# A one-core encoder layer with experts: order of evacuations, signals and idle products in the last attention steps and the last expert unit

## The chip, the core and the metric

The kernel runs on one core of one Trainium2 chip. The metric is the device time of the program in microseconds (us), lower is better. Five engines work beside each other, each through its own instructions in order: TensorE (PE, with its weight loads PEld), VectorE (DVE), ScalarE (ACT), GpSimd (POOL) and SyncE (SP), which here only issues transfers. They meet through semaphores: an instruction adds to one when it is done, another engine waits until the count is reached.

## What is computed

One layer on 1024 tokens of width 1024, in float32: a mixing part (four mLSTM heads, eight attention heads over a sliding window, one output projection), then a mixture of sixteen experts.

```python
x = x + jnp.concatenate([hm, ha], axis=-1) @ w_out[l]      # hm: mLSTM heads, ha: attention heads
x = x + hier_moe(rmsnorm(x, norm_ffn[l]), ...)             # top-1 group, top-2 experts in it
return rmsnorm(x, norm_final)
...
for e in range(N_EXPERTS):                                 # in hier_moe
    y = (jax.nn.silu(xt @ w_gate[e]) * (xt @ w_up[e])) @ w_down[e]
    out = out + combine[:, e:e + 1] * y
```

## The kernel before

**Products.** A float32 product is made of three rounded ones (`split3`, L1944 to L1946): both operands are split into a high part, which ScalarE writes as a rounded copy, and a low part, which VectorE writes as the difference. So every operand passes ScalarE, then VectorE, before TensorE may use it.

**Mixing part, steps.** After the input projection and the attention, a loop of steps s = 0 to 10 runs on all engines, with NT = 8 tiles of 128 tokens. In step s the mLSTM of tile s, the output projection of tiles s-2 (second 512 columns, `project(s-2, 1)`) and s-1 (first 512, `project(s-1, 0)`) and the router of tile s-3 go on. In `project(c, half)` the attention part comes first (`project_attention`: high rows AQH, made by `attention_hi(c)` on ScalarE at L1006, and low rows AQL, made by `attention_lo(c)` on VectorE at L1402), then from step 3 on the router's product `logits(c-2)` (L2152), then the mLSTM part (HTH from ScalarE at L1082, HTL from VectorE). In each step ScalarE first copies the two halves of the router's transposed rows (`router_evac`, L633; TensorE makes the second half only after `project(s-2, 1)`), then HTH, then AQH of tile s-1; further down it squares a tile for the norm (L1091) and the mLSTM's output (`sq`, L1096). VectorE waits in order for AQL, then adds a projection half to the residual (L1505), then makes HTL. Steps 7 and 8 have less TensorE work than those ahead: step 7 is the last with an mLSTM output and updates no state, step 8 does neither.

**From router to units.** After the last step VectorE makes tables of which token goes to which expert, in short steps that depend on each other (L1523 to L1564, L1659 to L1711); its last instruction, L1711, signals `s_tab`. TensorE fills waits with `keep_busy(n)`, n products of 128x128 that nobody reads (`ones` by the identity, L2231; each shows as two matmuls in the trace), reads two numbers of the table, transposes the first unit's rows (`x_half`, L2239) and begins the first unit's products.

**Expert units.** The sixteen units (at most 256 rows each, up to two halves of 128) each take six weight pieces of 1 MB: four for gate and up, j = 0 to 3, two for down, j = 4 and 5. SP loads a piece into RAW, ScalarE makes WH (L1069), VectorE makes WL (L1669, in the last unit L1733), TensorE multiplies. Three slots of WH and WL are used in turn, and `s_wused` counts the pieces that TensorE is through with. A unit's second half can be empty, full, or hold at most 64 rows ("few"): then both parts of these rows share one product (L2264, L2266). In this run the last unit has few rows in its second half.

**The last unit** is written apart. After piece j = 3 (up) come: ScalarE moves the lower half of the second half's up products (`low_rows(3)`, L1129 for SG); VectorE adds it (`both_rows`, L1766), multiplies by gate and silu (L1906 for the second half, `times_up(0, 1)`, L1772, for the first); TensorE transposes the hidden rows (L2308); ScalarE and VectorE split them into HH and HL (L1125, L1758); TensorE does piece j = 4 for both halves (12 matmuls each), adds the gathered rows of the tokens' sums by the identity (`add_rows`, L2396), and does piece j = 5. Beside this SP loads the eight tiles of 512 KB of the sum from device memory (`acc_dram`, L760), ScalarE squares them (L1235), VectorE scales them (L1919), SP stores them (L764), and at the very end POOL scatters the last unit's own rows over them (L931), in two halves, after all eight stores have landed.

Of the kernel before, what the change touches and what calls it, by code (L numbers as in the profile page):

```python
# [98 lines left out]
def build(nc, x, norm_mix, w_in, b_in, conv_qk, mlstm_norm, sinks, rel_bias, w_out, norm_ffn,  # L99
# [14 lines left out]
    with ctx:  # L114
# [822 lines left out]
        def _(act):  # L937
# [133 lines left out]
            for s in range(NT + 3):  # L1071
                if 3 <= s < NT + 2:
                    router_evac(act, s - 3, 0)
                    router_evac(act, s - 3, 1)
                if s == NT + 1:
                    router_evac(act, NT - 1, 0)
                    router_evac(act, NT - 1, 1)
                if 1 <= s <= NT:
                    act.wait_ge(s_ht, s)
                    if s >= 2:  # L1080
                        act.wait_ge(s_wo, 2 * s - 2)
                    A((hT0 if s == 1 else HTH)[:, :, :], PS[:, 3, :].rearrange("p (a b) -> p a b", a=4),  # L1082
                      ACT.Copy).then_inc(s_hte, 1)
                    if s >= 2:
                        attention_hi(s - 1)
                if 2 <= s < NT + 2:
                    c = s - 2
                    act.wait_ge(s_x2, 2 * c + 2)
                    if c >= 1:
                        act.wait_ge((s_xnst1, s_xnst0)[c % 2], 16 * ((c + 1) // 2))  # L1090
                    A(xnb[:, :], VM[:, c, 0:D], ACT.Square, accum_out=stat[:, c:c + 1]).then_inc(s_ss2, 1)  # L1091
                if s == NT + 1:
                    hi_piece(0, 0)
                if s < NT:
                    act.wait_ge(s_num, s + 1)
                    A(sq[:, 0:3, :], num3[:, :, 0:P], ACT.Square).then_inc(s_sq, 1)  # L1096
                if s + 1 < NT:
                    decays(s + 1)
                    scales(s + 1)
                if s == 1:  # L1100
                    act.wait_ge(s_wout, 32)
                    act.wait_ge(s_mog, 8)
                    for i in range(2):
                        A(WMH[i][:, :, :], wout[:, 2 * i:2 * i + 2, :], ACT.Copy).then_inc(s_wmh, 1)
# [117 lines left out]
            with act.If(second > 0):  # L1222
                with act.If(second < 2):
                    act.wait_ge(s_wused, 6 * u + 3 + SPLITS)
                    low_rows(2).then_inc(s_glo, 1)
                    gate_tanh(0).then_inc(s_th, 1)
                    act.wait_ge(s_gsum, 2 * u + GSUM + 1)
                    A(SG[0:FEW, 1, :], HB[0:FEW, 1, :], ACT.Tanh, scale=0.5).then_inc(s_th, 1)
                    act.wait_ge(s_wused, 6 * u + 4 + SPLITS)
                    low_rows(3).then_inc(s_glo, 1)  # L1230
# [5 lines left out]

            hi_piece(u, 5)
            for i in range(NT):
                if i == 2:
                    hi_piece(u, 6)  # L1240
                    hidden_hi(u, 0, 1)
                    hidden_hi(u, 1, 0)
                act.wait_ge(s_vm[i], 32)
                square(i, tile_of(i))
            act.wait_ge(s_dn1, u + 1)
            act.wait_ge(s_f2a, NT)
# [8 lines left out]
        def _(dve):  # L1255
# [616 lines left out]
            def both_times_up():  # L1872
                dve.wait_ge(s_sil, 2 * u + 2)
                dve.wait_ge(s_gate, 32 * u + 32)
                dve.wait_ge(s_wused, 6 * u + 4 + SPLITS)
                for hf, bank in ((1, 3), (0, 1)):
                    times_up(hf, bank).then_inc(s_hb, 1)

# [5 lines left out]
            with dve.If(second > 0):  # L1884
                with dve.If(second < 2):
# [7 lines left out]
                                           ALU.add, ALU.mult).then_inc(s_sil, 1)  # L1893
            last_lo_piece(u, 5)
            with dve.If(second > 1):
# [3 lines left out]
            with dve.If(second > 0):  # L1899
                with dve.If(second < 2):  # L1900
# [5 lines left out]
                    V.scalar_tensor_tensor(HB[0:FEW, 1, :], HB[0:FEW, 1, :], gt[0:FEW, 1:2], SG[0:FEW, 1, :],  # L1906
                                           ALU.mult, ALU.mult).then_inc(s_hb, 1)
                    times_up(0, 1).then_inc(s_hb, 1)
            hidden_lo(u, 0, 1)
            hidden_lo(u, 1, 0)  # L1910
# [24 lines left out]
        def _(pe):  # L1935
# [319 lines left out]

            def second_gate_up(par, j, slot, full):
                with pe.If(full > 0):
                    with pe.If(full > 1):
                        gate_up(par, j, slot, 1)
                    with pe.If(full < 2):  # L2260
                        for k in range(4):
# [3 lines left out]
                               start=(kk == 0), stop=False)  # L2265
                            mm(PS[:, 2 + j % 2, :], both_parts, WLS[slot][:, F * k:F * k + F],  # L2266
                               start=False, stop=(kk == KD - 1))

# [92 lines left out]

            keep_busy(6)
            pe.wait_ge(s_tab, 1)
# [7 lines left out]
            x_half(0, 0, 0).then_inc(s_xt, 1)  # L2371
            x_half(1, 0, 0).then_inc(s_xt, 1)
            pe.wait_ge(s_xl, 2)
            pe.wait_ge(s_wlo, 1)
# [15 lines left out]
            for j, slot in ((1, 1), (2, 2), (3, 0)):  # L2390
                pe.wait_ge(s_wlo, 6 * u + j + 1)
                second_gate_up(par, j, slot, second)
                gate_up(par, j, slot, 0).then_inc(s_wused, 1)
# [49 lines left out]
```

## Time and profile before

| | us |
|---|---|
| median of 3 runs | 951.76 |
| lowest and highest | 950.52, 952.11 |
| the profiled execution's own time | 950.21 |
| its span, first to last instruction | 947.9 |
| TensorE busy in the span | 902.6 |
| VectorE, ScalarE, GpSimd busy in the span | 667.6, 455.4, 293.0 |

Times in the rows are counted from the span's start. A bracket at a row's end is the time in which that engine stood idle just before, and what ended it. "PEclk" is the share of TensorE's full clock (2.4 GHz) that was granted: 1.00 or 0.50. The steps end at about 480 us, the table is ready at about 499 us, and the units' products run from 503 to 939 us.

### The profile page before, as it was taken

How to read it: one execution, taken by the hardware profiler on the slowest of the kernel's cores; microseconds unless marked ns; L12 is line 12 of the kernel's file. 1: busy time of each engine (PE TensorE's matmuls, PEld its weight loads, DVE VectorE, ACT ScalarE, POOL GpSimd, SP SyncE). 2: the span in 40 equal slices, each digit the busy share in tenths (PEclk: the TensorE clock that was granted, in tenths of full speed). 3: DMA queues.
4: the chain of work that ended last, by engine and by line, in shares of the span. 5: the costliest groups of instructions: out<-in, count | busy, mean ns of one | idle time of the engine just before them, and what ended most of it. 6: DMA issues, size and time to landing. Idle time of an engine off the chain costs nothing.

```text
span 947.9 us, 16162 instructions
## 1 busy us (share of the span) xinstructions
PE 902.6 (95%) x4934; PEld 751.4 (79%) x4935; DVE 667.6 (70%) x1156; ACT 455.4 (48%) x717; POOL 293.0 (31%) x307
## 2 busy tenths in 40 slices
PE   8999999999999999999878999999999999999966
PEld 7888788888888778888666777888888778787754
DVE  7872447576675988677588888775566776787756
ACT  7422334253443533232135776564546656666653
POOL 1300000000000011001015888454344766594444
PEclk9999999999999999999968999999999999999988
DMA  8531103030203752123448999987778897999856
GB/s 303 150 90 45 45 23 112 24 90 22 68 23 100 213 199 90 67 84 118 189 185 300 344 377 376 354 263 226 236 234 258 267 365 256 315 311 316 256 188 265
DMA packets 86199, 183.56 MB, mean 194 GB/s; under 512 B 8395, under 2 KB 29216, under 8 KB 86146
## 3 DMA queue, kind: packets, MB, share of 16 engines
q1 hardware_dynamic: 76114, 153.48, 46.5%
q0 software_dynamic: 9872, 29.32, 11.7%
q8 instruction: 31, 0.51, 0.2%
q14 instruction: 22, 0.18, 0.1%
q10 hardware_dynamic: 160, 0.07, 0.0%
HBM read 150.89 MB, written 31.40 MB: 192 GB/s over the span
## 4 chain that ended last, share of the span: by engine, by line
PE 84%; DVE 7%; issue 3%; ACT 3%; DMA 1%; POOL 0%; SPq 0%; DVEq 0%; POOLq 0%; ACTq 0%
PE PS L1944 21%; PE PS L1946 20%; PE PS L1945 20%; PE PS L2264 3%; PE PS L2266 3%; PE PS L2239 2%; PE PS L2293 1%; PE PS L2294 1%; PE PS L2152 1%; PE PS L2302 1%; DMA XT<-in_x_dram 1%; DVE WP L593 1%; PE PS L2077 1%; PE PS L2051 1%; PE PS L1952 1%
## 5 line engine op out<-in xcount | busy, mean ns | idle before, releaser
L1669 DVE TENSOR_TENSOR WL<-RAW,WH 128x2048 fp32r<-128x2048 f32 x94 | 214.1, 2289 | 46.2 <-ACT WH L1069 46.0
L1069 ACT ACTIVATE WH<-RAW 128x2048 fp32r<-128x2048 f32 x96 | 183.8, 1914 | 29.7 <-PE PS L1946 17.0
L1944 PE MATMUL PS<-WH,XH 128*128 128x512 f32 x288 | 118.0, 410 | 2.9 <-DVE XL L1738 1.3
L1946 PE MATMUL PS<-WH,XL 128*128 128x512 f32 x288 | 113.6, 394 | 0.0
L1945 PE MATMUL PS<-WL,XH 128*128 128x512 f32 x288 | 113.2, 393 | 0.0
L808 POOL TENSOR_TENSOR dst<-dst,stat 128x4 f32<-128x4 f32 x8 | 8.2, 1020 | 319.7 <-DVE dst L1626 319.7
L816 POOL TENSOR_TENSOR stat<-stat 128x1 f32<-128x1 f32 x107 | 71.8, 682 | 58.2 <-ACT YB L1179 40.2
L1944 PE MATMUL PS<-HNH,WP 128*128 128x512 f32 x208 | 84.2, 405 | 1.6 <-issue 1.6
L1946 PE MATMUL PS<-HNH,WP 128*128 128x512 f32 x208 | 81.9, 394 | 0.0
L1945 PE MATMUL PS<-HNL,WP 128*128 128x512 f32 x208 | 81.8, 393 | 0.0
L1944 PE MATMUL PS<-WP,HNH 128*128 128x256 f32 x256 | 73.6, 288 | 0.0
L1945 PE MATMUL PS<-WP,HNH 128*128 128x256 f32 x256 | 72.2, 282 | 0.0
L1946 PE MATMUL PS<-WP,HNL 128*128 128x256 f32 x256 | 72.1, 282 | 0.0
L1944 PEld LDWEIGHTS PS<-WH,XH 128*128 128x128 f32 x288 | 54.6, 189 | 15.4 <-issue 5.5
L1946 PEld LDWEIGHTS PS<-WH,XL 128*128 128x128 f32 x288 | 54.5, 189 | 12.1
L1944 PE MATMUL PS<-WH,HH 128*128 128x512 f32 x152 | 61.0, 401 | 2.7 <-DVE HL L1758 1.8
L1945 PEld LDWEIGHTS PS<-WL,XH 128*128 128x128 f32 x288 | 54.6, 189 | 9.8
L1946 PE MATMUL PS<-WH,HL 128*128 128x512 f32 x152 | 59.7, 393 | 0.0
L1945 PE MATMUL PS<-WL,HH 128*128 128x512 f32 x152 | 59.7, 393 | 0.0
L840 POOL DMA_INDIRECT gt<-comb_dram,gixc x30 | 52.2, 1740 | 8.1 <-issue 7.3
L1108 ACT ACTIVATE XH<-PS 128x256 fp32r<-128x256 f32 (+2 forms) x64 | 28.8, 456 | 50.4 <-PE PS L2239 49.6
L824 POOL DMA_INDIRECT acc_dram<-YB,idsc x23 | 48.6, 2115 | 6.8 <-issue 6.8
(385 smaller groups left out, 2072.9 us busy)
## 6 DMA issues: line engine op xcount, KB each, us to landing
RAW<-in_w_gate_dram SPq DMA_DIRECT2D x32, 1024.0 KB, 7.6
RAW<-in_w_up_dram SPq DMA_DIRECT2D x32, 1024.0 KB, 12.2
RAW<-in_w_down_dram SPq DMA_DIRECT2D x32, 1024.0 KB, 6.6
wraw<-in_w_in_dram SPq DMA_DIRECT2D x22, 512.0 KB, 4.3
XT<-in_x_dram SPq DMA_DIRECT2D x8, 512.0 KB, 6.9
vo_dram<-vo SPq DMA_DIRECT2D x16, 256.0 KB, 2.1
wout<-in_w_out_dram SPq DMA_DIRECT2D x4, 1024.0 KB, 7.8
VM<-vo_dram SPq DMA_DIRECT2D x16, 256.0 KB, 5.6
```

The source lines that it names most:

```text
L816: nc.gpsimd.tensor_tensor(stat[:, col:col + 1], stat[:, 32:33], stat[:, 32:33], ALU.add)
L824: nc.gpsimd.indirect_dma_start(acc_dram, bass.IndirectOffsetOnAxis(ap=idsc[:, hf:hf + 1], axis=0), YB[:, hf, :], None, compute_op=ALU.add) ...
L840: nc.gpsimd.indirect_dma_start(gt[:, hf:hf + 1], None, comb_dram, bass.IndirectOffsetOnAxis(ap=rows[:, hf:hf + 1], axis=0)).then_inc(s_gat ...
L1069: A(WH[:, d % SPLITS, :], RAW[:, j, :], ACT.Copy).then_inc(s_whi, 1)
L1108: A(XH[:, par, 2 * g:2 * g + 2, 0:n], PS[:, 6 + g % 2, :].rearrange("p (a b) -> p a b", a=2)[:, :, 0:n], ACT.Copy).then_inc(s_xh, 1)
L1669: V.tensor_tensor(WLS[d % SPLITS][:, :], RAW[:, TURN[d][1] if d else 0, :], WH[:, d % SPLITS, :].bitcast(fp32), ALU.subtract).then_inc(s_w ...
L1944: mm(bank, ah, bh, start=start, stop=False)
L1945: mm(bank, ah, bl, start=False, stop=False)
L1946: return mm(bank, al, bh, start=False, stop=stop)
L2239: last = tr(PS[:, 6 + g % 2, UNIT * k + P * hf:UNIT * k + P * hf + P], XGS[par][:, hf, P * (2 * g + k):P * (2 * g + k) + P], ident)
L2264: mm(PS[:, 2 + j % 2, :], both_parts, WH[:, slot, F * k:F * k + F], start=(kk == 0), stop=False)
L2266: mm(PS[:, 2 + j % 2, :], both_parts, WLS[slot][:, F * k:F * k + F], start=False, stop=(kk == KD - 1))
```

## The change

The change has four parts.

- **Attention rows ahead.** `attention_hi(s-1)` on ScalarE stands between the two router copies of the step, no longer behind HTH.
- **A signal for half of a piece.** In the last unit, `second_gate_up` at j = 3 adds 1 to `s_dn1` when the second half's up products are done, so `low_rows(3)` on ScalarE and `times_up(1, 3)` on VectorE wait for that and no longer for the whole piece (`s_wused`). The later user of `s_dn1`, ScalarE's square of the second half's result, waits for one more.
- **VectorE's and ScalarE's order in the last unit.** VectorE does the products with up ahead of the low part of piece j = 4. ScalarE splits the hidden rows right after the high part of piece 4, then makes the high part of piece 5, and squares tiles only then (before: two squares and piece 5 came ahead of the hidden rows).
- **Idle products.** `keep_busy(6)` ahead of the wait for the table becomes `keep_busy(10)`, and `keep_busy(5)` is new behind the first unit's transposes.

```diff
@@ ScalarE, steps @@
                 if 3 <= s < NT + 2:
                     router_evac(act, s - 3, 0)
+                if 2 <= s <= NT:
+                    attention_hi(s - 1)
+                if 3 <= s < NT + 2:
                     router_evac(act, s - 3, 1)
...
                     A((hT0 if s == 1 else HTH)[:, :, :], PS[:, 3, :].rearrange("p (a b) -> p a b", a=4),
                       ACT.Copy).then_inc(s_hte, 1)
-                    if s >= 2:
-                        attention_hi(s - 1)
@@ ScalarE, last unit @@
-                    act.wait_ge(s_wused, 6 * u + 4 + SPLITS)
+                    act.wait_ge(s_dn1, u + 1)
                     low_rows(3).then_inc(s_glo, 1)
...
             hi_piece(u, 5)
+            hidden_hi(u, 0, 1)
+            hidden_hi(u, 1, 0)
+            hi_piece(u, 6)
             for i in range(NT):
-                if i == 2:
-                    hi_piece(u, 6)
-                    hidden_hi(u, 0, 1)
-                    hidden_hi(u, 1, 0)
                 act.wait_ge(s_vm[i], 32)
                 square(i, tile_of(i))
-            act.wait_ge(s_dn1, u + 1)
+            act.wait_ge(s_dn1, u + 2)
@@ VectorE, last unit @@
                 dve.wait_ge(s_gate, 32 * u + 32)
+                dve.wait_ge(s_dn1, u + 1)
+                times_up(1, 3).then_inc(s_hb, 1)
                 dve.wait_ge(s_wused, 6 * u + 4 + SPLITS)
-                for hf, bank in ((1, 3), (0, 1)):
-                    times_up(hf, bank).then_inc(s_hb, 1)
+                times_up(0, 1).then_inc(s_hb, 1)
...
-            last_lo_piece(u, 5)
             with dve.If(second > 1):
                 both_times_up()
...
+                    dve.wait_ge(s_wused, 6 * u + 4 + SPLITS)
                     times_up(0, 1).then_inc(s_hb, 1)
+            last_lo_piece(u, 5)
             hidden_lo(u, 0, 1)
             hidden_lo(u, 1, 0)
             last_lo_piece(u, 6)
@@ TensorE @@
-            def second_gate_up(par, j, slot, full):
+            def second_gate_up(par, j, slot, full, done=0):
                 with pe.If(full > 0):
                     with pe.If(full > 1):
-                        gate_up(par, j, slot, 1)
+                        last = gate_up(par, j, slot, 1)
+                        if done:
+                            last.then_inc(s_dn1, done)
...
-            keep_busy(6)
+            keep_busy(10)
             pe.wait_ge(s_tab, 1)
...
             x_half(1, 0, 0).then_inc(s_xt, 1)
+            keep_busy(5)
             pe.wait_ge(s_xl, 2)
...
-                second_gate_up(par, j, slot, second)
+                second_gate_up(par, j, slot, second, 1 if j == 3 else 0)
+                if j == 3:
+                    with pe.If(second < 1):
+                        nc.tensor.sem_inc(s_dn1, 1)
```

ScalarE in a late step, from the router's second copy of the step to the square, before:

```order
L633 ACTIVATE xnT<-PS 128x512 x2
L1082 ACTIVATE HTH<-PS 128x512
L1006 ACTIVATE AQH<-aqT 128x512
L1091 ACTIVATE xnb,stat<-VM 128x1024
L633 ACTIVATE xnT<-PS 128x512 x2
L633 ACTIVATE xnT_last<-PS 128x512 x2
```

and in the changed kernel:

```order
L633 ACTIVATE xnT<-PS 128x512
L1006 ACTIVATE AQH<-aqT 128x512
L633 ACTIVATE xnT<-PS 128x512
L1085 ACTIVATE HTH<-PS 128x512
L1092 ACTIVATE xnb,stat<-VM 128x1024
L633 ACTIVATE xnT<-PS 128x512 x2
```

The attention rows (AQH) moved from behind HTH to between the two halves of the router's rows (xnT).

TensorE between the table's last product (L2235) and the first unit's transposes (XG holds the gathered rows, `cst` by `ones` are the idle products), before:

```order
L2235 MATMUL PS<-acu,ones 128x85
L2231 MATMUL PS<-cst,ones 128x128 x6
L2364 TENSOR_LOAD tab
L2364 ISA x2
L2312 TENSOR_LOAD tab
L2312 ISA x2
L2366 COMPARE_AND_BRANCH
L2239 MATMUL PS<-cst,XG 128x128 x4
L2366 UNCONDITIONAL_BRANCH
L2239 MATMUL PS<-cst,XG 128x128 x4
```

and in the changed kernel, with two more lines of code ahead, so that L2235 is L2237:

```order
L2237 MATMUL PS<-acu,ones 128x85
L2233 MATMUL PS<-cst,ones 128x128 x10
L2370 TENSOR_LOAD tab
L2370 ISA x2
L2318 TENSOR_LOAD tab
L2318 ISA x2
L2372 COMPARE_AND_BRANCH
L2241 MATMUL PS<-cst,XG 128x128 x4
L2372 UNCONDITIONAL_BRANCH
L2241 MATMUL PS<-cst,XG 128x128 x4
L2233 MATMUL PS<-cst,ones 128x128 x5
```

Four idle products more stand ahead of the two reads of the table, and five behind the transposes.

VectorE in the last unit, path for few rows, from the silu of the few rows on (WL_144 is the low part of piece 4, WL_142 of piece 5), before:

```order
L1892 SCALAR_TENSOR_TENSOR HB<-SG,HB 64x512
...
L1733 TENSOR_TENSOR WL_144<-RAW,WH 128x2048
...
L1766 TENSOR_TENSOR SG<-PS,SG 64x512
...
L1906 SCALAR_TENSOR_TENSOR HB<-HB,gt,SG 64x512
L1772 SCALAR_TENSOR_TENSOR HB<-HB,gt,PS 128x512
...
L1758 TENSOR_TENSOR HL<-PS,HH 128x4x128
...
L1758 TENSOR_TENSOR HL<-PS,HH 128x4x128
...
L1733 TENSOR_TENSOR WL_142<-RAW,WH 128x2048
```

and in the changed kernel:

```order
L1893 SCALAR_TENSOR_TENSOR HB<-SG,HB 64x512
...
L1766 TENSOR_TENSOR SG<-PS,SG 64x512
...
L1906 SCALAR_TENSOR_TENSOR HB<-HB,gt,SG 64x512
...
L1772 SCALAR_TENSOR_TENSOR HB<-HB,gt,PS 128x512
...
L1733 TENSOR_TENSOR WL_144<-RAW,WH 128x2048
...
L1758 TENSOR_TENSOR HL<-PS,HH 128x4x128
...
L1758 TENSOR_TENSOR HL<-PS,HH 128x4x128
...
L1733 TENSOR_TENSOR WL_142<-RAW,WH 128x2048
```

The low part of piece 4 went from ahead of the three products with up to behind them. ScalarE in the same place, before:

```order
L1228 ACTIVATE SG<-HB 64x512
...
L1129 ACTIVATE SG<-PS 64x512
...
L1069 ACTIVATE WH<-RAW 128x2048
L1235 ACTIVATE fjunk,fin<-VM 128x1024 x2
...
L1069 ACTIVATE WH<-RAW 128x2048
...
L1125 ACTIVATE HH<-PS 128x4x128
...
L1125 ACTIVATE HH<-PS 128x4x128
L1235 ACTIVATE fjunk,fin<-VM 128x1024 x5
```

and in the changed kernel:

```order
L1229 ACTIVATE SG<-HB 64x512
...
L1130 ACTIVATE SG<-PS 64x512
...
L1069 ACTIVATE WH<-RAW 128x2048
...
L1126 ACTIVATE HH<-PS 128x4x128
...
L1126 ACTIVATE HH<-PS 128x4x128
...
L1069 ACTIVATE WH<-RAW 128x2048
L1236 ACTIVATE fjunk,fin<-VM 128x1024 x7
```

The hidden rows (HH) and the high part of piece 5 went ahead of the first two squares (fjunk).

## Rows read from the trace of the kernel before

**Rows 1.** Timelines, steps 7 and 8: start, us, instruction [idle before <-releaser].

```profile
443.72 0.47 PE L1944 MATMUL PS<-woh_early,AQH 128*128 128x512 f32 x1 [0.29 <-DVE AQL L1402]
...
444.21 1.07 ACT L1091 ACTIVATE xnb<-VM 128x1024 f32<-128x1024 f32 x1 [1.36 <-DVE VM L1505]
...
445.84 0.69 DVE L1619 TENSOR_REDUCE dst<-sq 128x4 f32<-128x512 f32 x1 [0.47 <-ACT sq L1096]
...
452.10 0.63 PE L2138 MATMUL PS<-cst,VM 128*128 128x128 f32 x4 [0.81 <-DVE lg L1643]
...
459.67 0.63 ACT L1006 ACTIVATE AQH<-aqT 128x512 fp32r<-128x512 f32 x1
...
460.34 0.69 DVE L1402 TENSOR_TENSOR AQL<-aqT,AQH 128x512 fp32r<-128x512 f32 x1 [4.21 <-ACT AQH L1006]
...
461.18 0.47 PE L1944 MATMUL PS<-woh_early,AQH 128*128 128x512 f32 x1 [2.07 <-DVE AQL L1402]
```

**Rows 2.** Stretches: length, busy us (xinstructions) by engine, PEclk, DMA share, GB/s.

```profile
462.10:465.50 3.40, 3.40 (x10) 2.62 (x9) 0.13 (x1) 0.89 (x2) 0.74 (x2) 0.51 0.03 5
...
470.00:480.00 10.00, 9.20 (x55) 7.61 (x53) 9.65 (x37) 2.34 (x5) 0.00 (x0) 1.00 0.25 79
...
496.50:499.60 3.10, 2.88 (x13) 2.59 (x12) 2.88 (x13) 0.00 (x0) 0.13 (x1) 0.51 0.77 267
...
499.70:503.00 3.30, 0.98 (x5) 0.72 (x6) 2.70 (x4) 0.66 (x2) 2.64 (x4) 1.00 0.25 51
...
503.10:506.40 3.30, 3.30 (x9) 2.58 (x8) 3.18 (x9) 0.00 (x0) 0.66 (x2) 0.50 0.92 304
...
900.00:910.00 10.00, 10.00 (x46) 8.29 (x45) 4.13 (x3) 3.45 (x4) 7.08 (x9) 1.00 0.25 52
...
916.10:926.30 10.20, 5.16 (x16) 4.10 (x17) 8.08 (x9) 8.75 (x13) 0.70 (x2) 0.50 1.02 394
...
930.00:931.00 1.00, 1.00 (x5) 0.48 (x4) 1.00 (x3) 0.22 (x2) 0.11 (x1) 1.00 0.99 410
```

**Rows 3.** Timelines of PE and DVE, between the tables and the first unit.

```profile
496.45 2.93 PE L2231 MATMUL PS<-cst,ones 128*128 128x128 f32 x12
...
498.63 0.18 DVE L1711 TENSOR_SCALAR tab<-kk__178 128x28 int32<-128x28 f32 x1
...
500.71 0.66 PE L2239 MATMUL PS<-cst,XG 128*128 128x128 f32 x4 [1.33 <-issue]
...
502.67 0.56 PE L1944 MATMUL PS<-WH,XH 128*128 128x512 f32 x1 [1.30 <-DVE XL L1738]
```

**Rows 4.** Timelines of the last unit, of PE, ACT, DVE and POOL.

```profile
911.36 0.68 DVE L1892 SCALAR_TENSOR_TENSOR HB<-SG,HB 64x512 f32<-64x512 f32 x1
...
913.88 0.59 ACT L1129 ACTIVATE SG<-PS 64x512 f32<-64x512 f32 x1 [2.56 <-PE PS L1946]
...
914.50 1.91 ACT L1069 ACTIVATE WH<-RAW 128x2048 fp32r<-128x2048 f32 x1
...
915.59 0.95 POOL L921 DMA_INDIRECT XG<-acc_dram,idxc  x1 [0.30 <-issue]
...
916.44 2.29 DVE L1733 TENSOR_TENSOR WL<-RAW,WH 128x2048 fp32r<-128x2048 f32 x1 [4.40 <-ACT WH L1069]
...
920.37 1.97 PE L2308 MATMUL PS<-cst,HB 128*128 128x128 f32 x8 [6.52 <-DVE HB L1906]
...
923.11 0.79 PE L1944 MATMUL PS<-WH,HH 128*128 128x512 f32 x1 [0.77 <-DVE HL L1758]
...
930.13 3.59 PE L2396 MATMUL PS<-XG,cst 128*128 128x512 f32 x8
...
942.14 1.05 POOL L931 DMA_INDIRECT out_dram<-XG,idsc  x1 [0.35 <-issue]
```

**Rows 5.** DMA issues around 916.5 us: KB each, median us to landing.

```profile
last_tile<-acc_dram SPq DMA_DIRECT2D x1, 512.0 KB, 12.0
...
XG<-acc_dram,idxc POOLq DMA_INDIRECT x1, 9.5
```

More of the change, by code:

```diff
@@ L2265, in second_gate_up @@
                                start=(kk == 0), stop=False)
-                            mm(PS[:, 2 + j % 2, :], both_parts, WLS[slot][:, F * k:F * k + F],
-                               start=False, stop=(kk == KD - 1))
+                            last = mm(PS[:, 2 + j % 2, :], both_parts, WLS[slot][:, F * k:F * k + F],
+                                      start=False, stop=(kk == KD - 1))
+                        if done:
+                            last.then_inc(s_dn1, done)
             def down_bank(hf, half):
```

## The prediction

> **What bounds the kernel now.** I read the stretches first, for what TensorE does and at which clock. In an ordinary stretch of the units it is busy for all of 10.00 us, with 44 to 46 matmuls in it, one about every 0.227 us (the row from 900.00, [rows 2]). So the time is TensorE's, and a change counts where TensorE stands idle or runs at half clock, and at the two ends where another engine sets the pace. Then the timelines of the places that the diff touches. The reader should see four holes: short ones of 0.29 and 0.81 us in steps 7 and 8 and one of 2.07 us in step 8, the last behind the chain ScalarE AQH, VectorE AQL [rows 1]; a mostly idle 3.3 us ahead of the first unit, where TensorE works 0.98 us [rows 2]; and 6.52 us in the last unit [rows 4]. Behind three of them stands a stretch in which TensorE is busy at a granted clock of 0.50 to 0.51 (1.2 GHz), so that half of the stretch is lost once more [rows 2]. Last, the end: the first scatter of the last unit's rows starts at 942.14 [rows 4], behind TensorE's last product and behind the eight stores.
>
> **Attention rows ahead.** No instruction is added; seven copies of about 0.63 us change place. In step 8 TensorE has finished the transposes for HTH by 461.18 - 2.07 = 459.11 and then waits for AQL, which ends at 460.34 + 0.69 = 461.03; AQH itself ran from 459.67 [rows 1]. Moved ahead, AQH needs only the router's first copy, whose transposes start at 452.10; so it is done by about 454. VectorE has been idle since 460.34 - 4.21 = 456.13, so AQL is done by 456.8, over 2 us before TensorE wants it. The hole of 2.07 goes whole. What comes next for TensorE, twelve products of attention and sixteen of the router (4.5 us), hides HTH and HTL.
>
> The clock: from 462.10 to 465.50 it is 0.51 and TensorE is busy throughout [rows 2], right behind the hole. Without the hole TensorE doesn't pause there, so I expect the clock to stay up, as it is in full stretches, and 3.4 x 0.5 = 1.7 us come back.
>
> In step 7 the wait of 0.29 for AQL goes the same way. And VectorE's addition (VM, L1505), which stood behind AQL, comes earlier, so the square at 444.21 doesn't wait its 1.36 us, and the mLSTM's reduction at 445.84 not its 0.47. The router's logits at the end of that VectorE chain held TensorE for 0.81 us at 452.10 [rows 1]; a chain that begins 1.8 us earlier (1.36 + 0.47) covers that. Sum: 0.3 + 0.8 + 2.1 + 1.7 = 4.9 us. The other steps give nothing: there is more TensorE work between AQH and its reader. In step 2 the copy AQH goes ahead of HTH and delays it by 0.6 us; state products lie between HTH and its reader, so no cost.
>
> Does it carry to the table? Behind step 8 the time runs through VectorE (busy 9.65 of 10.00 us from 470 to 480, [rows 2]), whose chain starts at the router's product of tile 5 and meets only TensorE work that is also earlier. Low bound: if one hole reopens elsewhere and the clock falls anyway, 2.9 of the 4.9 are left.
>
> **Idle products.** Six took 2.93 us from 496.45 on, 0.49 us each at half clock [rows 3]; the clock was 0.51 there and full from 499.70 on [rows 2]. Four more end between 499.38 + 4 x 0.24 = 500.4 (full clock) and 499.38 + 4 x 0.49 = 501.3 (half); the transposes start at 500.71 anyway, since the table is there only at 498.63 + 0.18 = 498.81 and its two reads follow [rows 3]. Cost 0 to 0.6. The five behind the transposes stand in the 1.30 us wait for XL [rows 3]: 1.2 us at full, 2.4 us at half clock, so cost 0 to 1.1. The full clock is what the rows show for that place, so I take 0.1 in all. The gain: from 503.10 to 506.40 TensorE is busy for all of 3.30 us at 0.50, behind the mostly idle stretch [rows 2]. The nine products fill that stretch but for some tenths of a us, and nearly unbroken work is what stood ahead of the full clock at 499.70, so I expect it to be kept: 1.65 us back, net 1.5. Bounds: -1.7 to 1.6.
>
> The rows show that reading the table begins no later than the table; they don't show whether queued products would hold the reads back. The Trainium skill ("TensorE: Matmul & The Clock Gate", Architectural detail) gives TensorE a queue of 64 entries, and ten products are 20 matmuls and 20 weight loads; by that rule the reads aren't held. Were they held until the last product had run, the transposes would begin at 500.4 + 1.33 = 501.7 by the gap ahead of 500.71, 1.0 us later, and the net were 0.5.
>
> **The last unit.** The piece j = 3 ends at 913.88 - 0.03; its last twelve matmuls belong to the first half, so the second half's up products are done at 913.85 - 12 x 0.227 = 911.1. ScalarE's `low_rows(3)` (0.59) then runs to 911.95, as the tanh ahead of it ends by 911.36, and VectorE's silu ends at 911.36 + 0.68 = 912.04. VectorE's two operations for the second half, about 0.7 each, end at 913.6, so TensorE transposes it with hardly a pause; `times_up(0, 1)` runs 913.9 to 914.6, the second transposes end at 915.2. The high part of piece 4 (1.91) runs 912.0 to 913.9 on ScalarE instead of from 914.50, but VectorE does its low part (2.29) only behind the products, 914.6 to 916.9, and then HL of the second half to 917.6 [rows 4]. That is the late one now: the hidden rows are there, the low parts are not. Piece 4 starts at about 917.8, before 923.11: 5.3 us earlier. Piece 5's low part ends at 920.5, long before its use.
>
> **What is late next** is no arithmetic but transfers. First the gathered rows: the second gather is issued at 915.59 and lands 9.5 us later, at 925.1 [rows 4, 5]. TensorE reaches `add_rows` at 917.8 + 24 x 0.227 = 923.2, or 924.9 if the pause ahead of it costs as much as the half clock from 503.10 on (1.65). Both are before 925.1: the clock's gain there is hidden, and `add_rows` starts at about 925.1, before 930.13, 5.0 us earlier. By this chain the first scatter comes at 937.1. Second the stores: the last tile's load, issued at about 916.7, lands 12.0 us later at 928.7 [rows 5], and eight stores of 0.524 MB at the 410 GB/s of a full stretch (the row from 930.00, [rows 2]) take 1.28 us each, 10.2 us, to 938.9. In the kernel before, scaling paced the stores; now five tiles are scaled by 928.7 and the stores run back to back behind the loads on SP's queue. With 0.4 to the scatter it starts at 939.3, not at 942.14: 2.8 us, and the second scatter no longer waits for VectorE, 0.2 more. I take 3.0. Bounds: 1.5 (stores mix with loads, and the last tile is scaled late) to 5.0 (the stores don't bind).
>
> That stores wait behind the loads is inferred, since no row has both at once. The Trainium skill ("DMA: Bandwidth & Descriptors", Queues, rings and completion order) says that each transfer engine takes one queue's descriptors in ring order, which is that case; either way the bytes are the same, so the two differ by little at the end.
>
> **Sum.** 4.9 + 1.5 + 3.0 = 9.4 us. The profiled execution took 950.21 and would take 940.8. It is 1.55 below the median 951.76, which I take as base: 942.4.
>
> **Rivals.** *The idle products give nothing* (the clock falls all the same, or they hold the transposes): 1.5 is lost, to 3.2 at the worst; 942.4 + 1.5 to 3.2 = 944 to 945.6. For it: some pauses are left around the transposes, and no row shows such a mix. *The units absorb the start*: if the transfers of weights and gathers pace the units in places, the 6.4 us won ahead of them shrink; all of it gone gives 951.76 - 3.0 = 948.8. Against it: TensorE is full [rows 2]. *The end follows TensorE*: the stores don't bind, 5.0 in place of 3.0: 940.4. *The end binds harder*: 1.5 in place of 3.0: 943.9. *Slower*: the units start earlier against transfers whose times are their own (the gathers of the next rows by POOL, 9.5 us from issue to landing in a full stretch [rows 5]). If TensorE then waits in each of the sixteen units, it decides from 9.4 / 16 = 0.6 us a unit; at 1.0 us a unit the time is 951.76 - 9.4 + 16 = 958.4. Against it: no wait of that kind stands in the full stretch [rows 2], and POOL is released by the same engines that come earlier. *It doesn't do what it says*: if the last unit had no few rows, the order would act otherwise; the rows of the path for few rows are in the trace (L1892, [rows 4]), so I give that nothing of its own.
>
> **How the numbers follow.** Forecast 0.60; idle products without gain 0.12; end binds harder 0.10; end follows TensorE 0.07; start absorbed 0.07; slower 0.03; no change 0.01. The forecast's own terms reach from 938.5 (951.76 less 5.2 + 1.6 + 5.0, and 1.5 for runs that differ, as these three do by 1.6) to about 945. The range 938.5 to 946.5 takes in the first three rivals and leaves out the last ones, near 0.12. A difference under 0.2% (1.9 us) can't be told from no change here. Faster 0.96, same 0.01, slower 0.03.
>
> **What would show it.** Right, if the profile after shows: no wait of TensorE for AQL and a clock of 1.00 up to the router's last products; the first unit's twelve matmuls at 0.23 us each; a gap of 2 to 3 us instead of 6.5 ahead of piece 4, then one of up to 2 us ahead of `add_rows`, ended by the gathered rows; and stores back to back up to the scatter. Wrong, if the half clock appears at 503 all the same, if piece 4 waits longer, or if TensorE waits in the units where it didn't.

## The result and the profile after

| | us |
|---|---|
| the changed kernel, median of 4 runs | 942.62 (942.42 to 943.49) |
| the kernel before beside it, median of 4 runs | 951.89 (950.52 to 952.11) |
| ratio, 95% interval | 0.9904 (0.9889 to 0.9920) |
| the profiled execution's own time, its span | 942.81, 940.9 |

The forecast was 942.4, within 938.5 to 946.5. A later set of six runs of the same kernel gave a median of 944.26 beside 952.23 of before (0.9917, 0.9898 to 0.9936). The ten runs together lie between 942.35 and 945.41.

The page of the changed kernel, its line of TensorE and of the granted clock in 40 slices:

```profile
PE 902.3 (96%) x4952; PEld 751.7 (80%) x4953; DVE 668.2 (71%) x1156; ACT 455.3 (48%) x717; POOL 297.2 (32%) x307
...
PEclk9999999999999999999979999999999999999998
```

TensorE is busy as long as before (902.6), in a span that is 7.0 us shorter. Stretches of the changed kernel (start:end, length, busy time of PE, PEld, DVE, ACT, POOL, granted clock, DMA share, GB/s):

```profile
440.00:462.00 22.00, 22.00 (x125) 18.84 (x123) 13.41 (x40) 4.82 (x9) 1.76 (x3) 1.00 0.73 263
462.00:465.50 3.50, 3.50 (x25) 3.19 (x24) 1.44 (x8) 1.15 (x2) 0.74 (x2) 1.00 0.00 0
...
914.00:917.00 3.00, 3.00 (x9) 2.33 (x8) 2.36 (x4) 2.82 (x5) 0.67 (x2) 0.51 1.01 391
```

These answer [rows 1] and the half-clock stretch of [rows 2]: the holes of 0.29, 0.81 and 2.07 us are gone, TensorE is busy for 22.00 of 22.00 us, and the clock behind them is 1.00 where it was 0.51. In the last unit the clock still falls once.

The start of the units on TensorE (start, busy us, operation; the bracket is the idle time ahead):

```profile
492.77 4.64 PE L2233 MATMUL PS<-cst,ones 128*128 128x128 f32 x20
497.20 0.81 PE L2241 MATMUL PS<-cst,XG 128*128 128x128 f32 x4
497.85 1.28 PE L2233 MATMUL PS<-cst,ones 128*128 128x128 f32 x10
499.30 0.49 PE L1946 MATMUL PS<-WH,XH 128*128 128x512 f32 x1 [0.18 <-issue]
499.64 0.40 PE L1947 MATMUL PS<-WL,XH 128*128 128x512 f32 x1
499.87 0.40 PE L1948 MATMUL PS<-WH,XL 128*128 128x512 f32 x1
```

and two of the first unit's matmuls in the kernel before:

```profile
503.46 0.63 PE L1946 MATMUL PS<-WH,XL 128*128 128x512 f32 x1
503.89 0.63 PE L1944 MATMUL PS<-WH,XH 128*128 128x512 f32 x1
```

Against [rows 3] the waits of 1.33 and 1.30 us are filled, and from the second on the first unit's matmuls start every 0.23 us (499.64 to 499.87) where they started every 0.43 us (503.46 to 503.89). An idle product is two of these instructions: 0.46 us at half clock, 0.26 at full.

The last unit of the changed kernel, by engine (PE, DVE, SP's queue, POOL):

```profile
910.64 0.66 PE L2314 MATMUL PS<-cst,HB 128*128 128x128 f32 x4 [0.24 <-DVE HB L1772]
...
913.67 0.49 PE L1946 MATMUL PS<-WH,HH 128*128 128x512 f32 x1 [2.37 <-DVE HL L1758]
...
920.82 3.61 PE L2406 MATMUL PS<-XG,cst 128*128 128x512 f32 x8
```

```profile
909.84 0.75 DVE L1772 SCALAR_TENSOR_TENSOR HB<-HB,gt,PS 128x512 f32<-128x512 f32 x1 [0.15 <-PE PS L1948]
910.51 2.28 DVE L1733 TENSOR_TENSOR WL<-RAW,WH 128x2048 fp32r<-128x2048 f32 x1
912.71 1.28 DVE L1758 TENSOR_TENSOR HL<-PS,HH 128x512 fp32r<-128x512 f32 x2
```

```profile
918.26 9.59 SPq L764 DMA_DIRECT2D out_dram<-VM  x7
```

```profile
931.97 0.54 POOL L926 TENSOR_TENSOR fin<-fin,stat 128x1 f32<-128x1 f32 x1 [1.46 <-DMA out_dram<-VM]
935.57 1.05 POOL L931 DMA_INDIRECT out_dram<-XG,idsc  x1 [3.06 <-issue]
936.92 0.99 POOL L931 DMA_INDIRECT out_dram<-XG,idsc  x1 [0.30 <-issue]
```

They answer [rows 4]: TensorE stands idle for 2.37 us ahead of piece 4, where before it waited 6.52 us ahead of the transposes of the hidden rows and 0.77 us behind them. GpSimd now stands idle for 3.06 us before the first scatter, where before it was 0.35.

### Where the 7 us lie

A shift is read from the start of the same instruction in two traces. Four places on VectorE cut the span into stretches: a product of the mLSTM ahead of everything that the change touches, the table, the hidden rows' low part in the second unit, and the first operation of the last unit's gating. In the kernel before:

```profile
344.60 0.68 DVE L1582 SCALAR_TENSOR_TENSOR qs<-ibc,qT 128x512 f32<-128x512 f32 x1
...
538.91 0.69 DVE L1758 TENSOR_TENSOR HL<-PS,HH 128x512 fp32r<-128x512 f32 x1
...
909.98 0.68 DVE L1766 TENSOR_TENSOR HB<-PS,SG 64x512 f32<-64x512 f32 x1 [4.54 <-ACT SG L1129]
```

and the table's row at 498.63 in [rows 3]. In the changed kernel:

```profile
346.29 0.68 DVE L1582 SCALAR_TENSOR_TENSOR qs<-ibc,qT 128x512 f32<-128x512 f32 x1
...
494.95 0.18 DVE L1711 TENSOR_SCALAR tab<-kk__178 128x28 int32<-128x28 f32 x1
...
535.33 0.68 DVE L1758 TENSOR_TENSOR HL<-PS,HH 128x512 fp32r<-128x512 f32 x1
...
905.93 0.68 DVE L1766 TENSOR_TENSOR HB<-PS,SG 64x512 f32<-64x512 f32 x1 [4.53 <-ACT SG L1130]
```

So the shift is +1.69, -3.68, -3.58 and -4.05 us, and -7.0 at the end of the span. By stretch: +1.69 before the change does anything, -5.37 up to the table, +0.10 in the first unit, -0.47 in the others, -2.95 in the last. The same for the profile of every kernel that ran (the sections below say what each is), as differences to the one profile of before:

| kernel | up to 344.60 | to the table | first unit | other units | last unit and end |
|---|---|---|---|---|---|
| attention rows alone | +3.47 | -5.38 | +1.29 | -0.27 | +0.49 |
| idle products alone | +1.71 | +0.02 | +0.77 | -0.11 | +1.11 |
| last unit alone | +0.06 | -0.04 | +1.57 | -0.20 | -2.29 |
| hole filled | +2.01 | -1.54 | +0.75 | -0.26 | +0.14 |
| rows and idle products | +0.31 | -5.37 | +0.14 | -0.49 | +0.91 |
| changed kernel | +1.69 | -5.37 | +0.10 | -0.47 | -2.95 |
| changed kernel, again | +2.00 | -5.38 | +0.73 | -0.33 | -2.02 |
| changed, half stores | -0.09 | -5.35 | +0.08 | -0.20 | -4.94 |
| changed, gates early | +0.03 | -5.34 | -0.72 | -0.10 | -2.17 |
| the same, again | +0.11 | -5.37 | -0.80 | -0.21 | -3.03 |
| gates early, no idle products | -0.35 | -5.40 | +1.19 | -0.17 | -2.07 |
| gates early, more idle products | +1.39 | -5.56 | +0.56 | +0.17 | -2.06 |
| before, half stores | +2.05 | +0.01 | +0.05 | -0.27 | +0.16 |

Two columns follow the change: the second, to 0.06 us in eight of the nine profiles with the attention rows ahead, and the last, which is 2.0 us or more below zero wherever the last unit's edits are in, though it varies by 1 us between profiles of the same code. The first is no part of it. It is a draw between executions: in the changed kernel's profile a half-clock stretch lies near 80 us, while TensorE is busy all the time. Kernel before, then the changed one, same stretch:

```profile
75.00:90.00 15.00, 15.00 (x81) 12.51 (x81) 5.81 (x15) 5.37 (x11) 0.00 (x0) 1.00 0.26 71
```

```profile
75.00:90.00 15.00, 15.00 (x74) 12.31 (x74) 5.43 (x15) 4.64 (x10) 0.00 (x0) 0.89 0.25 71
```

It shows in 6 of the 14 profiles, at about 1.6 us each, in kernels with and without the change. Two profiles (attention rows alone, and before with half stores) have another one at 335 to 340 us, mean clock 0.66 and 0.71, behind a stretch with pauses that the kernel before has too. The profile of before that the prediction was read from had neither, and its time, 950.21, is below those of the four runs beside it.

### The profile page after: what moved, and what is told of

It is laid out like the page before. It is cut to its first block, busy times and chain, and to the rows that moved or that the text cites. A ratio compares the mean times of both kernels' runs of the same rounds, so it can differ in the third digit from the quotient of the medians.

```text
span 940.9 us, 16200 instructions
## 1 busy us (share of the span) xinstructions
PE 902.3 (96%) x4952; PEld 751.7 (80%) x4953; DVE 668.2 (71%) x1156; ACT 455.3 (48%) x717; POOL 297.2 (32%) x307
## 4 chain that ended last, share of the span: by engine, by line
PE 77%; DVE 7%; issue 6%; DMA 4%; POOL 2%; ACT 2%; POOLq 1%; SPq 0%; DVEq 0%; ACTq 0%
PE PS L1946 19%; PE PS L1948 18%; PE PS L1947 18%; PE PS L2268 2%; PE PS L2270 2%; PE PS L2241 2%; PE PS L2154 1%; DMA XT<-in_x_dram 1%; DMA VM<-acc_dram 1%; DVE WP L593 1%; PE PS L2299 1%; PE PS L2300 1%; PE PS L2079 1%; PE PS L2308 1%; PE PS L2209 1%
```

## The experiments

The theory: the parts add up as forecast (attention rows 4.9, idle products 1.5, last unit 3.0), the stores set the end. The rivals: the idle products give nothing, the first units give the start's gain back, the end follows TensorE. Times are medians. A ratio is to the runs of before in the same set, whose medians were 951.84 (first four), 952.23 (second four) and 952.13 (third four).

### The parts alone

**Attention rows alone** (ScalarE's order only):

```diff
+                if 2 <= s <= NT:
+                    attention_hi(s - 1)
+                if 3 <= s < NT + 2:
                     router_evac(act, s - 3, 1)
...
-                    if s >= 2:
-                        attention_hi(s - 1)
```

> Only the attention rows of ScalarE stand ahead, idle products and last unit as before. The parts theory (each part's gain stands by itself): 4.9 us faster than before (946.9), of which 3.2 are waits of TensorE that go and 1.7 the half clock behind the 2.07 us wait. The rival that the first units give it back: 0 to 2 us faster, with longer waits for XL or HL in the first two units. If it gives more than 5.5, the half clock had cost more than 1.7.

Measured 947.71, ratio 0.9952 (0.9939 to 0.9965), so 4.1 by the medians and 4.6 by the ratio. The stretch up to the table is 5.38 us shorter in its trace. This is the largest part, it stands by itself, and at its place it is about half a us above the forecast's 4.9. The time gains less than that, and in this trace the first unit gives 1.29 us back.

**Idle products alone:**

```diff
-            keep_busy(6)
+            keep_busy(10)
...
+            keep_busy(5)
             pe.wait_ge(s_xl, 2)
```

> Only the nine idle products are added (10 in the place of 6, and 5 ahead of the wait for XL). The parts theory: 1.5 us faster (950.3), with the first unit's matmuls at full clock. The rival that queued products hold the transposes or the load of the table by their own time: 1.0 us slower to 0.3 faster. If the first units give part back, as the whole change's trace suggests: 0.5 to 1.0 faster.

Measured 951.82, ratio 1.0000 (0.9988 to 1.0013): no gain by time. The first unit ends 0.77 us later behind the table than in the profile of before, though its matmuls run at full clock. Its trace has a wait in the first unit that no row of before had:

```profile
519.21 0.75 DVE L1772 SCALAR_TENSOR_TENSOR HB<-HB,gt,PS 128x512 f32<-128x512 f32 x1 [1.74 <-DMA gt<-comb_dram,gix]
```

VectorE's product of the hidden rows (HB) with the gates (gt) waits for the gather of the gates. That is taken up below.

**Last unit alone** (all edits of the diff but the attention rows and the idle products; the core of it):

```diff
-                    act.wait_ge(s_wused, 6 * u + 4 + SPLITS)
+                    act.wait_ge(s_dn1, u + 1)
...
-            last_lo_piece(u, 5)
             with dve.If(second > 1):
                 both_times_up()
...
                     times_up(0, 1).then_inc(s_hb, 1)
+            last_lo_piece(u, 5)
```

> Only the last unit's edits (signal, VectorE's products ahead of the weight piece, ScalarE's pieces ahead of the squares). The parts theory: 3.0 us faster (948.8), set by the loads and stores of the final stretch and not by TensorE, which ends about 5.4 earlier relative to the rest. The rival that the end follows TensorE: 5 us faster. The rival that the last unit gains only together with the start: under 1.

Measured 948.92, ratio 0.9959 (0.9945 to 0.9974): 2.9 by the medians, 3.9 by the ratio. The last stretch takes 2.0 to 3.0 us less than in before's profile in each of the seven profiles with these edits and full stores, and 0.1 to 1.1 more in the five others with the old last unit; the means (-2.37, and +0.47 with before itself at 0) differ by 2.8. The last unit gains by itself, as forecast.

**The hole filled.** The kernel before, with eight idle products where TensorE waits 2.07 us for the last attention rows:

```diff
                     last.then_inc(s_ht, 1)
+                    if s == NT:
+                        for _ in range(8):
+                            mm(PS[:, 2, 0:P], ones[:, :], ident, start=True, stop=True)
```

> Before, and eight idle products in the 2.07 us that TensorE waits in step 8 for the last attention rows: no wait goes, only the idleness. If that wait is what lowers the clock behind it (462.1 to 465.5 at half): 1.7 us faster (950.1). If the half clock comes from the idleness of the whole stretch or of the waits ahead of it (0.29, 0.81), it stays: 0, or 0.1 slower by the products.

Measured 950.24, ratio 0.9983 (0.9974 to 0.9992): 1.6 us. TensorE at that place, and the stretches around it:

```profile
460.96 1.95 PE L2200 MATMUL PS<-cst,ones 128*128 128x128 f32 x16
463.19 0.47 PE L1944 MATMUL PS<-woh_early,AQH 128*128 128x512 f32 x1 [0.29 <-DVE AQL L1402]
```

```profile
458.00:462.00 4.00, 4.00 (x28) 3.55 (x27) 0.14 (x1) 1.28 (x3) 0.00 (x0) 1.00 1.04 382
462.00:466.00 4.00, 3.71 (x21) 3.06 (x20) 1.89 (x3) 1.48 (x3) 0.53 (x2) 1.00 0.17 66
```

The products of attention start no earlier than before, since AQL is as late as it was. Only the idleness is gone, and with it the half clock. So of the 5.4 us of the attention rows, 1.5 to 1.6 are the clock and the rest is waits that went.

### The start together, and the gates

**Attention rows and idle products**, the last unit as before (the first two diffs):

> Attention rows ahead and the nine idle products, the last unit as before. The parts theory by the forecast: 6.4 us faster than before (945.4). If the idle products give nothing because the gates' gather holds the first unit: as with the attention rows alone, 4.1 us faster (947.7). In its trace the wait of VectorE's HB for the gathered gates is 1 to 2 us by both.

Measured 946.41, ratio 0.9944 (0.9926 to 0.9962): 5.8 by the medians, between the two theories; 0.8 beyond the attention rows alone by the ratios, which the intervals don't tell from nothing.

**The changed kernel again**, as the measure for its neighbours:

> The changed kernel once more, as the measure for the runs beside it and for a second profile. If the extra half-clock stretch near 80 us in its first profile was a draw and not the change's, it may be absent or lie elsewhere now: span 939.2 without it, 940.9 with it; median 942.6 either way. Both theories of the first unit expect DVE's products by the gates to wait for the gates' gather here, 1 to 2 us.

Measured 944.26, ratio 0.9917 (0.9898 to 0.9936). Its profile was 2.0 us later again before anything that the change touches.

**Gates early.** Why the idle products gave so little: in the kernel before VectorE's product with the gates started 516.75 - 498.63 = 18.12 us behind the table and waited for TensorE. Before, then changed:

```profile
509.14 0.95 POOL L840 DMA_INDIRECT gt<-comb_dram,gix  x1 [0.30 <-issue]
...
516.75 0.75 DVE L1772 SCALAR_TENSOR_TENSOR HB<-HB,gt,PS 128x512 f32<-128x512 f32 x1 [0.25 <-PE PS L1946]
```

```profile
505.79 2.52 POOL L840 DMA_INDIRECT gt<-comb_dram,gix  x1 [0.30 <-issue]
...
513.12 0.75 DVE L1772 SCALAR_TENSOR_TENSOR HB<-HB,gt,PS 128x512 f32<-128x512 f32 x1 [1.19 <-DMA gt<-comb_dram,gix]
```

Changed: 513.12 - 494.95 = 18.17 us behind the table, now waiting for the gates. So it is in all five profiles with idle products and late gates (a wait of 1.16 to 1.85 us for the gates), while in all five without the idle products it waits for TensorE. The second gather lands 7.1 us after its issue in the changed kernel, at 512.9 or 17.9 us behind the table, and 6.4 us after it in the kernel before, at 515.5 or 16.9 behind. So the gates also come 1.0 us later behind the table than before; the gather itself takes GpSimd 2.52 us where it took 0.95, and why isn't shown. The gathers wait for indices that VectorE works out behind a weight piece of 2.3 us. What TensorE wins in piece 0 is waited for here. The test puts the indices ahead of that piece:

```diff
-            lo_piece(0, 1)
             scatter_rows()
+            lo_piece(0, 1)
```

> The changed kernel, and in VectorE's order the indices for the gates (scatter_rows) stand ahead of the weight piece that they waited behind (2.3 us). If the late gates take back what the idle products win: GpSimd's gathers of the gates start about 2.3 us sooner, the 1.19 us wait of HB goes and the time falls by 0.8 to 1.3 us against the changed kernel (941.5). If the first unit is set by VectorE's weight pieces or by the transfers instead: the wait goes and the time stays, or rises by up to 0.5, since weight piece 1 is split 1.2 us later.

Measured 942.17 beside 944.26, ratio 0.9902 (0.9883 to 0.9920). In its trace:

```profile
501.87 1.85 POOL L840 DMA_INDIRECT gt<-comb_dram,gix  x1 [0.30 <-issue]
...
510.71 0.75 DVE L1772 SCALAR_TENSOR_TENSOR HB<-HB,gt,PS 128x512 f32<-128x512 f32 x1 [0.49 <-PE PS L1948]
```

The product starts 510.71 - 493.32 = 17.39 us behind the table and waits for TensorE again. Its first unit is 0.82 us shorter than the changed kernel's first profile, 1.45 than its second. Once more:

> The kernel with the gates' indices ahead of the weight piece once more, as the measure for the two beside it: 942.2, with the wait of HB for the gathered gates gone in its second profile too.

Measured 943.26, ratio 0.9908 (0.9889 to 0.9928), again without that wait and with a first unit at -0.80. The eleven runs of this version have a median of 942.69, the ten of the changed kernel 943.15. So the traces show that the gates held the product back, and by time the version is at best slightly faster.

**Gates early, no idle products** (`keep_busy(6)` and none ahead of the wait for XL, the low part of the unit's input rows):

> The same kernel without the nine idle products (6 in the place of 10, none ahead of the wait for XL). If the late gates were what hid the idle products' gain: with the gates early, taking the products out costs the 1.5 us of the forecast (943.7). If the idle products win nothing by themselves: within 0.3 of the kernel with them. In the trace: from the table to the second unit, 0.9 to 1.6 us more than with them.

Measured 943.13, ratio 0.9911 (0.9892 to 0.9929), the same as with them by the medians. In the traces the first unit is 1.19 - (-0.80) = 2.0 us longer without them. The one profile and the six runs don't say the same, so what the idle products are worth with early gates stays open between 0 and 2.

What varies where there are none is the clock ahead of the first unit. In the kernel before the transposes ahead of it ran at full clock (0.66 us, [rows 3]). In the last unit alone, whose code up to there is the same and whose time up to there is the same to 0.02 us, they didn't:

```profile
500.70 1.11 PE L2240 MATMUL PS<-cst,XG 128*128 128x128 f32 x4 [1.31 <-issue]
```

Its first unit takes 1.57 us more. Of the five such profiles the two whose transposes took 0.66 us stand at 0 and 0.05, the three with 1.11 or 1.12 at 0.75 to 1.57. (These are the profiles without idle products and with late gates, before among them.) Their mean is 0.73; over the five with idle products and late gates it is 0.36, from 0.08 to 0.77. That is 0.4 us for the idle products, which the spread of five profiles each doesn't tell from nothing; what the rows do show is a narrower spread with them. The Trainium skill ("TensorE: Matmul & The Clock Gate", Part 1, the clock gate) says that the gate watches activity without regard to where a program begins, so the point at which the clock changes varies from run to run; these traces agree, with 0.66 and 1.11 us for the same four transposes.

### More idle products

Gates early, and idle products in the waits of the table stage too:

```diff
+            keep_busy(12)
             rank(EARLY, NT - EARLY, 3)
...
+            keep_busy(4)
             tables(range(2 * EARLY, 2 * NT)).then_inc(s_ix, 1)
...
-            keep_busy(4)
+            keep_busy(8)
...
-            keep_busy(10)
+            keep_busy(14)
```

> The same kernel, and more idle products in the waits of the table stage: 12 in TensorE's 4.2 us wait for VectorE's cum, 4 in its 1.6 us wait for high, 8 in the place of 4 and 14 in the place of 10 behind. If the clock then stays up there: the products between (rank 0.64, tables 1.83, counts 0.72, the gather's transposes 0.81 to 0.94 at half clock) take half, about 1.0 us faster (941.2). If the clock falls all the same, the queued products hold the real ones: 12 at half clock are 5.5 us in a wait of 4.2, so 1.3 slower or more.

Measured 944.90, ratio 0.9935 (0.9911 to 0.9958): 1.6 slower than its neighbour. TensorE, and two stretches:

```profile
480.02 4.52 PE L2228 MATMUL PS<-cst,ones 128*128 128x128 f32 x24
...
492.48 5.57 PE L2228 MATMUL PS<-cst,ones 128*128 128x128 f32 x28
497.89 0.60 PE L2243 MATMUL PS<-cst,XG 128*128 128x128 f32 x4
```

```profile
479.00:483.00 4.00, 4.00 (x25) 4.00 (x25) 3.41 (x18) 1.76 (x1) 0.00 (x0) 0.63 0.36 143
...
491.00:495.00 4.00, 4.00 (x19) 3.62 (x18) 3.59 (x21) 0.00 (x0) 1.14 (x2) 0.50 0.69 211
```

The clock fell in spite of TensorE being busy for 4.00 of 4.00 us, and the queued products then stood ahead of the transposes: the table was done at 494.46 + 0.18 = 494.64, and they started 3.25 us later, where it was 500.71 - 498.81 = 1.90 in the kernel before. The first three additions stand ahead of the table, and the table came no later for them (-5.56 in its column, -5.34 to -5.40 in the others). The delay behind it is then that of the last one, 14 in the place of 10: in its neighbour the transposes start 495.61 - 493.55 = 2.06 us behind the table. The profile shows 1.4 us lost in the first unit against its neighbour; the rest of the 1.6 may be draws.

### The end

**Half stores.** The changed kernel, storing only the left half of each final tile:

```diff
-                sp.dma_start(out2d[i * P:(i + 1) * P, :], tile_of(i)).then_inc((s_out0, s_out1)[i % 2], 16)
+                sp.dma_start(out2d[i * P:(i + 1) * P, 0:512], tile_of(i)[:, 0:512]).then_inc((s_out0, s_out1)[i % 2], 16)
```

> The changed kernel, but the final stores write only the left half of each of the eight tiles (2 MB less; that part of the output is left out). If the stores set the end, as forecast: the last scatters come up to 2.2 us sooner (to where the scaled last rows are ready), 940.4. If the end follows TensorE and the norm of the last rows: the scatters stay, within 0.3 of the changed kernel.

Measured 941.74 beside 944.26, ratio 0.9896 (0.9877 to 0.9916). Its scatters:

```profile
931.59 1.05 POOL L931 DMA_INDIRECT out_dram<-XG,idsc  x1 [0.35 <-issue]
933.39 0.99 POOL L931 DMA_INDIRECT out_dram<-XG,idsc  x1 [0.75 <-issue]
```

The last unit began 1.51 us earlier in this profile and the first scatter 3.98 earlier than in the changed kernel's, so the halved stores bring it forward by 2.47; GpSimd's wait of 3.06 ahead of it is back at the 0.35 of [rows 4]. Its last stretch stands at -4.94 in the table, where the two profiles of the changed kernel stand at -2.95 and -2.02. By time alone the intervals of the two overlap, so the reading rests on the traces: the stores set the end of the changed kernel. **The same in the kernel before:**

> The kernel before, with the same half stores (the right half of each of the eight tiles is left out). If the end of the kernel before is set by TensorE and the norm of the last rows, as forecast: within 0.3 of before. If its end too is set by the stores: 1 to 2.5 us faster.

Measured 952.28, ratio 1.0002 (0.9987 to 1.0017). Its first scatter keeps its pause:

```profile
944.12 1.05 POOL L931 DMA_INDIRECT out_dram<-XG,idsc  x1 [0.36 <-issue]
```

So the stores became the bound through the change, and were none before it.

## Why the prediction was right, and where it wasn't

- **Attention rows, 4.9 forecast.** Right in mechanism, short in size: 5.34 to 5.40 in eight profiles. The clock's share was 1.7 by the forecast and 1.5 to 1.6 with the hole filled; so it is the waits (3.2 forecast, 3.8 measured) that were undersized. Ahead of the hole of step 8 the shift grows by 1.64 us (from +1.69 at 344.60 to +0.05 at VectorE's rows near 449.60) where 0.3 and 0.8 were counted: 0.3 of it is there at 369 us already, in a step that was said to give nothing. Which of VectorE's waits holds the rest wasn't tested.
- **It carries to the table.** Right: the full shift of 5.37 stands at VectorE's row of the table.
- **Idle products, 1.5 forecast.** The step that failed. The matmuls of piece 0 ran at 0.23 us as forecast. But the gain was compared with one profile whose first unit had been short, and the sum took for granted that what TensorE wins in piece 0 is won for the whole unit: VectorE's product with the gates, which had started 18.12 us behind the table when TensorE was ready, started 18.17 us behind it, held by the gates' gather. What stayed is 0.4 us between the means of the traces, not told from nothing, and 0.0 alone by time. The rival "the idle products give nothing" named other reasons (the clock falling all the same, the transposes held) and gave them 0.12.
- **The units.** "TensorE is full" held: the other units take 0.1 to 0.5 us less than in before's profile in twelve of the thirteen others, in kernels with the old steps and without idle products too, so that is no gain of the change. The rival of absorption was right for one place that it didn't name, the first unit.
- **Last unit, 3.0 forecast.** Right. Set back by the 4.05 us by which this unit began earlier, piece 4 starts at 913.67 + 4.05 = 917.72 (917.8 forecast), `add_rows` at 924.87 (925.1), the first scatter at 939.62 (939.3). The forecast had `add_rows` wait for the gathered rows; the row at 920.82 shows no wait, since after a half-clock stretch (914 to 917) TensorE arrived as the rows had just landed (911.36 + 9.2 = 920.6). Three other profiles with these edits do show the wait: 1.38 us in the changed kernel's second one, 0.23 and 1.72 in two with the gates early. As the stores set the end, the clock's loss there cost nothing at the end, as forecast; no run tests that by itself.
- **The sum.** 9.4 forecast, 9.3 and 8.0 in the two sets. By term it is 5.4 + 0.4 + 2.8 = 8.6, and the three parts run alone add up to 4.1 + 0.0 + 2.9 = 7.0 by the medians and 4.6 + 0.0 + 3.9 = 8.5 by the ratios. The error of +1.1 in the idle products and that of -0.5 in the attention rows partly cancel, so the 0.2 us between forecast and first median is luck in part.
- **Base.** The profiled execution of before had drawn no half clock in its first 345 us and a short first unit. Other profiles had up to 3.5 and 1.6 us of these. With the profile's own time as base the forecast had been 940.8, 1.8 us below the first median and 3.5 below the second; the median of three runs as base took that out.

## What to carry to other kernels

A wait of 2 us on TensorE can cost nearly twice its length, because the clock falls behind it. Where an order of copies on another engine makes such a wait, changing the order gives back both. Before an idle stretch is filled for the clock's sake, ask what the work behind it will wait for next: here the gates' gather, 18 us behind the table. And a single profile can be 1.5 us lucky in a stretch of 40: compare each stretch over several executions before a gain of that size is counted.

## What the runs showed of the hardware that was not expected

- The clock went to half while TensorE was busy without a gap: 15.00 of 15.00 us at a mean of 0.89 in the changed kernel, 1.00 in the kernel before with the same instructions; in 6 of 14 profiles, about 1.6 us each.
- A row of idle products doesn't always keep the clock: 0.50 from 491 to 495 us with TensorE busy for all 4.00, but 1.00 behind the sixteen instructions in the filled hole.
- Halving the final stores (2 MB) brought the end forward by 2.5 us, not by the 5.1 that 2.1 MB take at the 410 GB/s of [rows 2]: then the norm of the last rows binds.
